# Last stage of a streaming-encoder layer: GpSimd's order becomes both low halves, wait for picks, gathers; VectorE's group begins with the gating

## The reference

```
def block(args):
    xx, ee, gg = args
    hid = jnp.einsum('td,tkd->tk', xx, u[ee].astype(jnp.float32))
    act = jax.nn.gelu(hid, approximate=False) * gg
    return jnp.einsum('tk,tkd->td', act, v[ee].astype(jnp.float32))
...
h_res = h_res + peer(rmsnorm(h_res, norm2_g[l]), ...)
```

## Time and profile before

| | us |
|---|---|
| median of 3 runs | 3891.9 |
| lowest and highest run | 3855.92, 3894.92 |
| span of the profiled execution | 3865.0 |
| TensorE (PE) busy | 3499.0 (91%) |
| VectorE (DVE) busy | 2644.0 (68%) |
| GpSimd (POOL) busy | 1996.7 (52%) |
| ScalarE (ACT) busy | 1277.0 (33%) |

### The profile page before, as it was taken

The page is one execution under the profiler, slowest core; times in us unless marked ns, Lnnn a source line. Parts: engine busy times, 40 slices in busy tenths (PEclk is TensorE's granted clock), DMA queues, the critical chain, the costliest instruction groups (busy, mean ns, idle before and its releaser), DMA issues. The chain is left out here.

```text
span 3865.0 us, 48416 instructions
## 1 busy us (share of the span) xinstructions
PE 3499.0 (91%) x17090; PEld 3027.2 (78%) x17090; DVE 2644.0 (68%) x4401; ACT 1277.0 (33%) x1926; POOL 1996.7 (52%) x1039
## 2 busy tenths in 40 slices
PE   7998989988998998998888889885899999999998
PEld 6886656667888998888888889885677777777776
DVE  2403668863116888777777777674888888888888
ACT  3222345642112224544444444543111111111111
POOL 3310000002102566666676666776677777777775
PEclk9997867779999999999899989987999999999999
DMA  3222000022223675666666656678777777777775
GB/s 117 101 82 94 22 12 12 12 103 88 60 64 131 197 237 170 204 214 199 207 202 204 204 201 202 219 262 286 281 252 266 265 258 268 261 262 266 256 273 202
DMA packets 302112, 697.30 MB, mean 180 GB/s; under 512 B 20704, under 2 KB 136288, under 8 KB 294752
## 3 DMA queue, kind: packets, MB, share of 16 engines
q1 hardware_dynamic: 228192, 426.35, 32.4%
q0 software_dynamic: 73728, 268.47, 20.5%
HBM read 564.72 MB, written 130.02 MB: 180 GB/s over the span
## 5 line engine op out<-in xcount | busy, mean ns | idle before, releaser
L855 POOL TENSOR_TENSOR u_lo<-u_raw,u_hi 128x1024 fp32r<-128x1024 f32 x128 | 375.6, 2934 | 443.5 <-ACT u_hi L800 443.1
L1890 PE MATMUL part<-v_hi,act_hi 128*128 128x512 f32 x1536 | 490.3, 401 | 107.8 <-POOL act_lo L1811 89.1
L1192 PE MATMUL hid_ps<-side_hi,u_hi 128*128 128x384 f32 x2048 | 558.0, 355 | 29.9 <-issue 18.1
L1829 DVE TENSOR_TENSOR acc<-acc,part 128x1024 f32<-128x1024 f32 x384 | 465.0, 1212 | 157.0 <-PE part L1890 131.4
L1192 PE MATMUL hid_ps<-side_lo,u_hi 128*128 128x384 f32 x2048 | 546.2, 349 | 0.0
L1192 PE MATMUL hid_ps<-side_hi,u_lo 128*128 128x384 f32 x2048 | 542.8, 347 | 0.0
L1890 PE MATMUL part<-v_lo,act_hi 128*128 128x512 f32 x1536 | 477.7, 392 | 0.0
L1120 DVE SCALAR_TENSOR_TENSOR found<-found,x_first 128x1024 f32<-128x1024 f32 x232 | 388.3, 1674 | 130.6 <-DMA found<-in_u,pick_now 129.7
L1890 PE MATMUL part<-v_hi,act_lo 128*128 128x512 f32 x1536 | 475.9, 391 | 0.0
L1890 PEld LDWEIGHTS part<-v_hi,act_hi 128*128 128x128 f32 x1536 | 281.0, 189 | 208.6 <-issue 119.9
L1838 DVE SCALAR_TENSOR_TENSOR acc<-found,pick_act,acc 128x1024 f32<-128x1024 f32 x256 | 443.0, 1769 | 0.0
(11 more groups left out here) (204 smaller groups left out, 6033.7 us busy)
## 6 DMA issues: line engine op xcount, KB each, us to landing
u_raw<-in_uT SPq DMA_DIRECT2D x128, 512.0 KB, 3.5
v_raw<-in_v SPq DMA_DIRECT2D x64, 1024.0 KB, 4.8
hid_d<-hid SPq DMA_DIRECT2D x128, 384.0 KB, 4.5
gate_d<-stage SPq DMA_DIRECT2D x48, 1024.0 KB, 7.1
act_in<-hid_d SPq DMA_DIRECT2D x64, 768.0 KB, 4.4
gate_in<-gate_d SPq DMA_DIRECT2D x64, 768.0 KB, 6.5
w_raw<-in_w_in SPq DMA_DIRECT2D x6, 2048.0 KB, 8.7
w_raw<-in_wq SPq DMA_DIRECT2D x4, 2048.0 KB, 8.8
```

The source lines that it names most:

```text
L855: pool.tensor_tensor(u_lo[:, s % 2], u_raw[:, :, :], u_hi[:, s % 2].bitcast(F), ALU.subtract).then_inc(u_lo_ok, 1)
L1192: mm = pe.matmul(hid_ps[:, s % 2, half, 0:W], w[:, s % 2, ch], x[:, ch, GB * P + half * W:GB * P + (half + 1) * W], start=n == 0, stop=n = ...
L1829: dve.tensor_tensor(acc[:, GB + n], acc[:, GB + n], part[:, n % BANKS], ALU.add).then_inc(added, 1)
L1890: last = pe.matmul(part[:, tb % BANKS, cols], a[:, s, j, rows], v[:, s, j, cols], start=m == 0, stop=m == len(passes) - 1)
```

## The change

GpSimd's order in a group becomes v_lo, a_lo, wait for the hand-out, gathers. (The added wait for `pick_ok` to be 1 is always met once the first hand-out is done.) VectorE's order becomes: gating of the next group, adds 0 and 1, first picks, adds 2 and 3, second picks, hand-out, adds 4 and 5. Nothing is computed differently.

```
@@ def low(p, s), GpSimd @@
                 g = 2 * p + s
-                pool.wait_ge(pick_ok, g + 1)
                 pool.wait_ge(v_hi_ok, g + 1)
                 pool.tensor_tensor(v_lo[:, s], v_raw[:, s], v_hi[:, s].bitcast(F),
                                    ALU.subtract).then_inc(v_lo_ok, 1)
+                pool.wait_ge(a_hi_ok, g + 1)
+                pool.tensor_tensor(a_lo[:, s], act_in[:, s], a_hi[:, s].bitcast(F),
+                                   ALU.subtract).then_inc(a_lo_ok, 1)
+                pool.wait_ge(pick_ok, 1)
+                pool.wait_ge(pick_ok, g + 1)
                 for n in range(PICK):
                     for b in range(GB):
                         pool.indirect_dma_start(found[:, s, b, n], None, v_d.rearrange("j i d -> (j i) d"),
                                                 bass.IndirectOffsetOnAxis(ap=pick_now[:, s, b, n:n + 1], axis=0))\
                             .then_inc(found_in[s][n], 16)
-                pool.wait_ge(a_hi_ok, g + 1)
-                pool.tensor_tensor(a_lo[:, s], act_in[:, s], a_hi[:, s].bitcast(F),
-                                   ALU.subtract).then_inc(a_lo_ok, 1)
@@ def body(p, first, last), VectorE @@
                     g = 2 * p + s
-                    adds(g, 0, 2)
                     if not (last and s == 1):
                         gates(p + s, 1 - s)
-                    adds(g, 2, 3)
+                    adds(g, 0, 2)
                     add_pick(p, s, 0, first and s == 0)
-                    adds(g, 3, 5)
+                    adds(g, 2, 4)
                     add_pick(p, s, 1, False)
-                    adds(g, 5, DENSE)
                     if not last:
                         hand_out(p + 1, s)
+                    adds(g, 4, DENSE)
```

## The result

The changed kernel is slower: the median is 3979.65 us (3977.34 to 3987.91, 4 runs) against 3887.69 of before (4 runs), a ratio of 1.0252 (1.0215 to 1.0289). Timed once more beside the last experiment it gave 3984.47 and 1.0321 (1.0303 to 1.0338), since the kernel before came out at 3862 that day; its median lay between 3862 and 3888 in all. The prediction had 3950 and +1.5%. The sign was right, and so was the loop that it priced. Its sum had +73 us; the spans of the two profiles differ by 110.5, and most of the other 37 come from something that it did not have, a VectorE copy caught behind a GpSimd subtraction.

The account below looks back on a forecast made before the run. It took a two-group loop of waits between VectorE, GpSimd and TensorE as the bound. The new loop's 19.21 us a group against 18.00, times 60, gave +73: span 3938, plus 13, stated as 3950 (3920 to 3985).

Parts of the forecast that it names:

- The old loop is cut: Last stage: cycle of hand-out, v_lo, gathers, a_lo, matmuls (35.80 us for two groups) ends; v_lo waits for v_hi alone.
- The wait for picks costs nothing in its new place: GpSimd, before the gathers: the hand-out comes a whole group ahead, so no cost; if wrong, cover is some 15 us.
- Gating and first picks wait for the subtractions: VectorE beside GpSimd subtractions, each group: gating held by v_lo (6.16 us to next VectorE start), first picks by a_lo (5.72).
- the prediction's third rival: VectorE's gating gets in before v_lo; the same period, 19.1 us, so counted with the forecast (together 0.80).
- The new loop, 38.41 for two groups, 19.21 each: Last stage, v_hi to v_hi two groups later: 19.21 us a group against 18.00, +73 us over 60 groups.
- add to matmul 1.26: From VectorE's fifth add to the next group's first matmul, which uses that add's bank: a new wait, 1.26 us.
- The hand-out at 0.07 us: VectorE's hand-out behind the second picks: 0.15 us less the overlap, 0.07 in the two-group sum.
- The clock: nothing: TensorE's clock drops after stops: bounds nothing and 51 us; nothing taken, since a late group found its inputs ready.
- the fourth rival: TensorE's clock drops at every long stop: up to 51 us more, time about 4002; chance 0.07.
- The launch and typical run: Median of before lies 27 us above the profiled span; half of it, 13, was added to the span of 3938.
- TensorE as the bound: If the port kept nobody waiting: TensorE's 16.4 us a group, 96 us less, about 3796; chance 0.05.
- Rival 2: Typical run of before sits mostly in 18.93 us periods, so only 17 us are lost: about 3909; chance 0.08.

Follow-up runs that it names:

- the last experiment: Changed kernel with 6 added matmuls in each group, placed where TensorE waits for the fifth add: 4036.47 us, ratio 1.0448 to the kernel before.
- the reduction: Changed kernel with the hand-out as a reduction over an axis of length 1 instead of a copy, same place and values: 3941.74 us, ratio 1.0190.
- the other run: Changed kernel with both the hand-out as a reduction and 12 added matmuls in each group: 3943.46 us, ratio 1.0200.
- the first of the two late-picks orders: Changed kernel with GpSimd's wait for picks ahead of v_lo; VectorE: gating, adds 0 to 4, first picks, add 5, second picks, hand-out: 3810.29 us, ratio 0.9855.

## Why the prediction was wrong in its size

Point by point, by its own steps.

- *The old loop is cut.* Right: the wait of 225 us is gone, v_lo starts 2.00 after v_hi (2.05 was the term), and TensorE waits 163.6 us for the fifth add, which the prediction named as new.
- *The wait for picks costs nothing in its new place.* Right: the gathers wait for no hand-out, and v_lo's 2.00 shows that they never delay it.
- *Gating and first picks wait for the subtractions.* Right in part: the gating took 4.80 and 5.88 at 3217.14 and 3236.56, the first two picks 4.83 and 5.20 at 3224.48 and 3244.63. Held are three gatings and five pairs of first picks in six groups; the other three gatings took 1.75. Two of them got in ahead of v_lo, as in the prediction's third rival, which it gave the same period (3159.99 and 3198.11; v_lo behind them took 5.38 and 6.09), and one came after v_lo's end, behind the caught hand-out (3261.03). "Each group", as its sign said, is wrong.
- *The new loop, 38.41 for two groups, 19.21 each.* Right, where it stands alone: 19.26 with neither caught hand-outs nor clock drops. With the reduction, where held and free gatings mix, it is 19.32; that run is 3942 against 3869 of before on the same chip, +73, and +73 was the sum (the other run gives +78). The pairs of one shorter and one longer period came out as sixes. Its new link, add to matmul 1.26, measures 3258.77 to 3260.03 = 1.26.
- ***The hand-out at 0.07 us*** is the term that failed. It was costed as free-running work. The prediction listed who needs the port (picks, gating, subtractions) and left out the copy, though the section of the Trainium skill that it cited, SBUF — State Buffer, "Who interferes with whom", names copies; in the trace of before the copy never met v_lo, since v_lo waited for it. The edit removed that wait, which was the very reason to ask. By its own loop the hand-out comes 20.43 us after v_hi and the next v_lo 19.21 + 2.05 = 21.26 after it, 0.8 apart, a margin it did not look at. Once in six groups v_lo was first, and the term measured 4.15 instead of 0.07. What it cost in all: mean period 19.80 instead of 19.32, 60 x 0.48 = 29 us; 34 by the spans (3975.5 against 3941.1), in which the start and end of the stage count too; about 40 by the medians, 3980 to 3984 against 3942.
- *The clock: nothing.* No direct cost showed in the loop (3942 with drops, 3943 without, as far as that run could show one), though the clock fell after nearly every long stop, which is the condition of the fourth rival. Its 51 us did not come: with the reduction the clock fell within the first nine matmuls behind 30 of 31 such stops, and the time was 3942. The drops may still have done the catching. A late TensorE by itself moves v_lo away from the hand-out; the group behind it can turn that round. In the trace the half clock after the stop at 3216.14 is followed by a v_lo 2.04 behind its hand-out (3234.18, 3236.22); the next v_lo comes only 18.04 later, the next hand-out 20.53. With drops gone no hand-out was caught. That they do the catching is likely and not shown: the added matmuls that keep the clock up move the phase as well.
- *The launch and typical run.* The span lies only 1.8 below its run's time (3977.34 and 3975.5), so of the 27 between span and median of before hardly anything was launch, and the half that was added was too much by 11. This went the other way and hid part of the miss.
- *The range.* 3980 lies inside the stated 3920 to 3985 by luck: its top was made of the slower median of before and of a cost of the clock, not of what happened. The change itself was +92 us where +58 was forecast.
- *Rivals.* TensorE as the bound was given 0.05 on the ground that the port always catches something. It is not so: with a suitable order TensorE is the bound, at 16.32. In this order it was out of reach. Rival 2, no change, fell too: the loss is clear even against the 3888 of the first comparison, and in the four later ones before stood at 3862 to 3869.

## What to carry to other kernels

When a wait is removed, ask what else it kept apart, not only what it delayed: list every operation on both engines that wants the same port, however small, and for each pair which now comes first and by what margin. A tiny operation that can be caught behind a long one should not stand ahead of what another engine waits for; give it a form that doesn't take the port, or a place where nothing urgent is behind it (here each brought the changed kernel from 3980 to about 3940). "Last" is no such place by itself: with GpSimd's order alone the hand-out stood last and was caught in every group. Put the long subtractions of GpSimd over the stretches in which VectorE reads PSUM; here such an order was worth 106 us against before.

## What the runs showed of the hardware

- A VectorE copy of four uint32 per partition waits for a whole GpSimd subtraction (4.15, 4.47 us), a reduction with the same tiles does not (0.16 beside it).
- The port goes to who asked first, and between two operations of one engine to the other if it waits: in the changed kernel all 21 a_lo asked for during a first pick ran behind it and ahead of the second, which then took 4.44 instead of 1.28. Behind the branch a gating 0.27 us behind v_lo took 5.95 instead of 1.76.
- GpSimd's indirect gathers are held as well, by a two-input VectorE operation that runs when they start: 2.30 at 3316.32 beside the gating, against 0.94. All 114 gathers of the changed kernel's stage that started in the middle of a pick (0.5 to 1.1 us ahead of its end) ended 0.81 to 0.84 after that pick; of the 103 that started during an add, which reads PSUM, none was held.
- Of the changed kernel's 31 stops of 1.5 us and more in the stage (2.37 to 7.96), TensorE came back from 30 at the half clock: the matmuls right behind them started 0.43 us apart, later ones 0.23. With the stops filled the granted clock stood at 1.00 from 2900 to 3500. It did so too in the first of the two late-picks orders, with 29 stops of 1.61 to 1.82 us, one in two groups.
- More TensorE work can shorten a kernel: 12 added matmuls a group gave -39 us, 6 gave +52.
